# Seven half-size block products in place of eight for the gate and up tiles of four feed-forward stages

## The chip, the cores and the metric

The program runs on one core of one Trainium2 chip. The metric is device time in microseconds for one execution, the median of several runs. Before the change it is 3092.79 us (3 runs, 3091.29 to 3094.11).

## The reference

The reference is a two-block transformer on one sequence of 512 tokens and width 1024, all in float32. The part that the change touches is the feed-forward network of the first block, which stands before and after the mixer in each of its two layers:

```
gate = x @ W_gate            # [512, 1024] @ [1024, 2816]
up   = x @ W_up              # [512, 1024] @ [1024, 2816]
h    = silu(gate) * up
x    = layer_norm(ALPHA * x + 0.5 * (h @ W_down))    # W_down: [2816, 1024]
```

The second block has two more feed-forward networks of the same sizes (with an RMS norm) and a mixer with sparse attention. They are left as they are. The result must agree with float32 to a tolerance that a single reduced-precision product doesn't meet.

## The kernel before, in words

**Layout.** Features are on the 128 partitions, tokens along the free dimension. `x` is [128, 8, 528]: 8 tiles of 128 features (index k), 16 meta columns and 512 tokens. A weight piece is 128 output features by 1024 input features (8 blocks of 128x128, one for each k), 512 KB. The hidden width 2816 is 22 tiles (index f, `FT`), so a feed-forward stage has 44 pieces for gate and up, in the order gate 0, up 0, gate 1, up 1, and then 24 for the down product (8 output tiles m of 3 pieces each).

**Precision.** Every operand is split in two: `hi` is the value rounded to the format that TensorE takes (fp32r), `lo` is the rest. Every block product is three matmuls: w_hi·x_hi (L397), w_lo·x_hi (L400), w_hi·x_lo (L403), all into one PSUM bank. A piece in these stages is 8 x 3 = 24 matmuls of 512 columns, each with its own weight load.

**Who does what for a piece.** SyncE loads it into one of four raw buffers (L379), as soon as the piece four before has been split. ScalarE copies it to `w_hi` (`act_split`, L340), VectorE takes the rest to `w_lo` (`dve_split`, L351); four slots hold the split pieces. For hidden tile f ScalarE takes silu of the gate bank (L574), VectorE multiplies with the up bank (L596), ScalarE makes the high part of h (L578) and VectorE its low part (L606). GpSimd has no work in the gate and up part of these stages; it adds squares and sums near the norms (L735, L754, L1031) and splits weights in the mixers (L366).

**Order.** Each engine runs one fixed list of instructions, written out by the loops in `ffn_pe`, `ffn_act`, `ffn_dve`; semaphores carry the dependencies. Step s of these loops is one piece; splits run three pieces ahead (`AHEAD`). The first 3 or 5 pieces of a stage are taken together (`pe_group`) while the norm before still delivers x. `Prepare` makes small tables of the second block beside the first stage.

The stages by the trace of before: first-layer feed-forward `ffn1_0` 0 to 387 us, `mix_0`, `ffn2_0` from 617, `ffn1_1` from 992, `mix_1` from 1366, `ffn2_1` from 1598, and the second block from 1985.

## Time and profile before

| | |
|---|---|
| median of 3 runs | 3092.79 us |
| span of the profiled execution | 3090.1 us |
| TensorE matmul busy | 3043.6 us (98%), 16494 matmuls |
| VectorE busy | 1421.9 us (46%) |
| ScalarE busy | 1158.2 us (37%) |
| GpSimd busy | 379.7 us (12%) |
| moved by DMA | 269.62 MB, mean 87 GB/s |

The profiled execution is told by its span, from its first to its last instruction; the median of the timed runs is 2.7 us above that span. A matmul's record overlaps the next one, since the array is pipelined: what a matmul costs is the distance between the starts of two that follow each other, not its duration. The same holds to a smaller degree for VectorE and ScalarE, where the next instruction starts some 0.09 us before the record of the last one ends. "Idle before" with a name behind it says what ended a wait.

### The profile page before, as it was taken

Reading aid. Unit: us, or ns where it says so; the run is one execution under the profiler, and the core shown is the slowest. Engines: PE = TensorE matmul, PEld = TensorE weight load, DVE = VectorE, ACT = ScalarE, POOL = GpSimd, SP = SyncE. Lnnn points to the kernel's source line nnn. Section 1 sums busy time; section 2 is a strip of 40 time slices with the busy share of each in tenths; the row PEclk is TensorE's granted clock in tenths of the full one; section 3 lists DMA queues with packets and bytes.
Section 4 is the critical chain, followed back from the end, with each engine's and each line's share of the span. In section 5 each row is a group of like instructions: output and inputs, shape, how many; then the busy total and the mean of one; then the engine's idle time right before and its main releaser. Section 6 shows DMA issues by size and latency. Waiting matters only on the chain.

```text
span 3090.1 us, 39392 instructions
## 1 busy us (share of the span) xinstructions
PE 3043.6 (98%) x16494; PEld 2548.2 (82%) x16494; DVE 1421.9 (46%) x2120; ACT 1158.2 (37%) x1868; POOL 379.7 (12%) x319
## 2 busy tenths in 40 slices
PE   9999999999999999999999999899999999999999
PEld 7888877888888888887788888899999767788888
DVE  4333465653335333356583333744423766554432
ACT  3322376442223322146553221522223456543221
POOL 0000143300001000014320000200002323200000
PEclk9999999999999999999999999999999999999999
DMA  4223331132332322332123223222233211122232
GB/s 161 96 94 89 93 103 62 55 110 96 94 93 66 117 95 92 94 118 67 55 76 103 95 90 95 75 96 89 86 89 102 80 38 35 41 95 93 93 93 77
DMA packets 76496, 269.62 MB, mean 87 GB/s; under 512 B 8720, under 2 KB 9008, under 8 KB 76064
## 3 DMA queue, kind: packets, MB, share of 16 engines
q1 hardware_dynamic: 74448, 260.08, 26.3%
q0 software_dynamic: 1872, 7.04, 0.7%
q8 instruction: 130, 2.13, 0.3%
q14 instruction: 46, 0.38, 0.0%
HBM read 264.97 MB, written 2.11 MB: 86 GB/s over the span
## 4 chain that ended last, share of the span: by engine, by line
PE 90%; DVE 7%; ACT 2%; issue 1%; DMA 0%; SPq 0%; POOL 0%; DVEq 0%; ACTq 0%
PE psum L397 25%; PE psum L400 25%; PE psum L403 25%; PE psum L461 3%; PE psum L473 2%; PE psum L416 1%; PE psum L420 1%; PE psum L418 1%; PE psum L696 1%; PE psum L2840 1%; DVE z_sum L853 1%; DVE x L865 1%; DVE x L858 1%; DVE b_rank L3115 0%; PE psum L1881 0%
## 5 line engine op out<-in xcount | busy, mean ns | idle before, releaser
L351 DVE TENSOR_TENSOR w_lo<-w_raw,w_hi 128x1024 fp32r<-128x1024 f32 (+1 forms) x444 | 554.7, 1251 | 1260.5 <-ACT w_hi L340 1260.4
L397 PE MATMUL psum<-x_hi,w_hi 128*128 128x512 f32 (+1 forms) x2800 | 964.0, 368 | 1.1 <-ACT neg_mean L2911 0.8
L400 PE MATMUL psum<-x_hi,w_lo 128*128 128x512 f32 (+1 forms) x2800 | 949.8, 363 | 0.9 <-DVE w_lo L351 0.9
L403 PE MATMUL psum<-x_lo,w_hi 128*128 128x512 f32 (+1 forms) x2800 | 945.2, 362 | 0.1
L340 ACT CAST w_hi<-w_raw 128x1024 fp32r<-128x1024 f32 (+1 forms) x490 | 503.7, 1029 | 1172.7 <-PE psum L403 1137.1
L397 PEld LDWEIGHTS psum<-x_hi,w_hi 128*128 128x128 f32 x2800 | 500.0, 188 | 109.0 <-issue 18.6
L400 PEld LDWEIGHTS psum<-x_hi,w_lo 128*128 128x128 f32 x2800 | 499.6, 188 | 88.0 <-issue 4.8
L403 PEld LDWEIGHTS psum<-x_lo,w_hi 128*128 128x128 f32 x2800 | 500.4, 189 | 84.7 <-DVE x_lo L3349 0.4
L397 PE MATMUL psum<-h_hi_ffn,w_hi 128*128 128x512 f32 (+1 forms) x792 | 296.9, 375 | 0.0
L400 PE MATMUL psum<-h_hi_ffn,w_lo 128*128 128x512 f32 (+1 forms) x792 | 292.2, 369 | 0.0
L403 PE MATMUL psum<-h_lo_ffn,w_hi 128*128 128x512 f32 (+1 forms) x792 | 290.7, 367 | 0.0
L397 PEld LDWEIGHTS psum<-h_hi_ffn,w_hi 128*128 128x128 f32 x792 | 149.0, 188 | 28.6 <-issue 1.0
L403 PEld LDWEIGHTS psum<-h_lo_ffn,w_hi 128*128 128x128 f32 x792 | 148.8, 188 | 28.2
L400 PEld LDWEIGHTS psum<-h_hi_ffn,w_lo 128*128 128x128 f32 x792 | 148.6, 188 | 27.2 <-issue 1.0
L366 POOL TENSOR_TENSOR w_lo<-w_raw,w_hi 128x512 fp32r<-128x512 f32 x92 | 119.7, 1324 | 248.6 <-ACT w_hi L340 248.5
L397 PE MATMUL psum<-h_hi_b_ffn,w_hi 128*128 128x264 f32 (+2 forms) x550 | 148.6, 316 | 0.0
L400 PE MATMUL psum<-h_hi_b_ffn,w_lo 128*128 128x264 f32 (+2 forms) x550 | 148.1, 315 | 0.0
L403 PE MATMUL psum<-h_lo_b_ffn,w_hi 128*128 128x264 f32 (+2 forms) x550 | 147.7, 314 | 0.0
L1031 POOL TENSOR_TENSOR z_sum<-x 128x512 f32<-128x512 f32 x4 | 5.2, 1299 | 1054.7 <-DVE x L1003 1054.7
L578 ACT CAST h_hi_ffn<-hid 128x512 fp32r<-128x512 f32 x88 | 54.6, 621 | 163.8 <-DVE hid L596 163.8
L403 PEld LDWEIGHTS psum<-h_lo_b_ffn,w_hi 128*128 128x128 f32 x550 | 93.2, 188 | 7.1
L397 PEld LDWEIGHTS psum<-h_hi_b_ffn,w_hi 128*128 128x128 f32 x550 | 93.1, 188 | 7.0
(386 smaller groups left out, 3388.3 us busy)
## 6 DMA issues: line engine op xcount, KB each, us to landing
w_raw<-in_ffn_gu SPq DMA_DIRECT2D x176, 512.0 KB, 3.3
w_raw<-in_ffn_down SPq DMA_DIRECT2D x64, 512.0 KB, 3.5
w_raw<-in_w_in SPq DMA_DIRECT2D x44, 512.0 KB, 3.3
w_raw<-in_b_gate SPq DMA_DIRECT2D x44, 512.0 KB, 3.3
w_raw<-in_b_up SPq DMA_DIRECT2D x44, 512.0 KB, 3.3
w_raw<-in_b_down SPq DMA_DIRECT2D x32, 512.0 KB, 3.5
w_raw<-in_ffn_down SPq DMA_DIRECT2D x32, 384.0 KB, 3.1
w_raw<-in_b_in SPq DMA_DIRECT2D x24, 512.0 KB, 3.3
```

Of the source, the lines that this page charges most:

```text
L340: nc.scalar.copy(w_hi[s][:, 0:n], w_raw[r][:, 0:n]).then_inc(*w_high.inc(u))
L351: nc.vector.tensor_tensor(w_lo[s][:, 0:n], w_raw[r][:, 0:n], w_hi[s][:, 0:n].bitcast(F32), ALU.subtract).then_inc(*w_low_dve.inc(u))
L366: nc.gpsimd.tensor_tensor(w_lo[s][:, c], w_raw[r][:, c], w_hi[s][:, c].bitcast(F32), ALU.subtract).then_inc(*w_low_pool.inc((u, half)))
L397: nc.tensor.matmul(out, w_h, hi[:, c], start=first and i == 0, stop=False)
L400: nc.tensor.matmul(out, w_l, hi[:, c], start=False, stop=False)
L403: done = nc.tensor.matmul(out, w_h, lo[:, c], start=False, stop=final and i == n - 1)
L416: nc.tensor.matmul(out, w_h, hi[:, c], start=j == 0, stop=False)
L418: nc.tensor.matmul(out, w_l, hi[:, c], start=False, stop=False)
L420: done = nc.tensor.matmul(out, w_h, lo[:, c], start=False, stop=j == KT // 2 - 1)
L461: nc.tensor.matmul(out, w_h, x_part[:, c], start=first, stop=False, skip_group_check=True)
L473: done = nc.tensor.matmul(out, w_l, x_hi[:, k, c], start=False, stop=k == KT - 1, skip_group_check=True)
L578: nc.scalar.copy(h_hi[:, f - 1, cols], hid[(f - 1) % 2][:, cols]).then_inc(*h_high.inc(f - 1))
```

## The change

In the four feed-forward stages of the first block the hidden tiles f = 4 to 21 no longer compute gate and up by two pieces of full width. The input is cut into its first and second four k (1, 2), the tokens into two halves of 256 (a, b), and the weights of a tile pair into G1, G2 (gate) and U1, U2 (up). The four results are made from seven products instead of eight, each of 4 x 3 = 12 matmuls of 256 columns:

```
s1 = U1+U2    s2 = s1+G1    s4 = s2+G2    s3 = U1+G1            (VectorE, per f)
n1 = x1a-x1b  n2 = -n1-x2b  t3 = x2b-x1b  t4 = -n2-x2a          (VectorE, once per stage)
m1 = G1 x1a   m2 = G2 x2a   m3 = s4 x2b   m4 = U2 t4
m5 = s1 n1    m6 = s2 n2    m7 = s3 t3
gate_a = m1+m2          gate_b = (m1+m6) + (m5+m3)
up_b = -(m1+m6+m7)-m5   up_a = -(m1+m6+m7+m4)
```

m1, m6, m7 and m4 are summed in one PSUM bank, and ScalarE copies that bank out between them (p1 after m1, p2 after m6); m5 and m3 are summed in a second one (copy r after m5). VectorE joins the parts (`gate_a`, `gate_b`, `up_b`) and makes the first half of h. GpSimd makes the second half of h and the low part of all of h, and after the last tile adds x_hi and x_lo back to x, since t3 and t4 are kept in x's own memory. The four split slots get roles: sums (s1 and s3), gate, up, later (s2 and s4). The raw buffer of a gate piece is free after s3, that of an up piece after its low part. `Prepare` moves to earlier steps and other buffers, and the memory for descriptors of GpSimd's DMAs is set to 4096 bytes.

```diff
+COMBINED = {"ffn1_0": 4, "ffn2_0": 4, "ffn1_1": 4, "ffn2_1": 4}
...
-                    sp.wait_ge(*w_low(u - RAW_SLOTS))
+                    last = u - RAW_SLOTS
+                    sp.wait_ge(*(raw_read[last] if last in combined else w_low(last)))
...
+            def pe_product(self, name, f):
+                role, at, block, b = {
+                    "m1": ("gate", 0, "gate", self.p_bank(f)),
+                    "m2": ("gate", 1, "gate", self.q_bank),
+                    "m3": ("later", 1, "later", self.r_bank(f)),
+                    "m4": ("up", 0, "up", self.p_bank(f)),
+                    "m5": ("sums", 0, "s1", self.r_bank(f)),
+                    "m6": ("later", 0, "later", self.p_bank(f)),
...
+                opens = name in ("m1", "m2", "m5")
...
+                for f in range(first, FT + 1):
+                    if f <= last:
+                        pe.wait_ge(*(self.joined.at(("gate_b", f - 2)) if f >= first + 2
+                                     else self.direct_left(self.r_bank(f))))
+                        self.pe_product("m5", f)
+                    if f > first:
+                        pe.wait_ge(*self.copied.at(("p2", f - 1)))
+                        self.pe_product("m7", f - 1)
+                    if f <= last:
+                        pe.wait_ge(*(self.first_half.at(f - 3) if f >= first + 3
+                                     else self.direct_left(self.p_bank(f))))
+                        self.pe_product("m1", f)
+                        pe.wait_ge(*(self.joined.at(("gate_a", f - 1)) if f > first
+                                     else self.direct_left(self.q_bank)))
+                        self.pe_product("m2", f)
+                    else:
+                        fill()
+                    if f > first:
+                        pe.wait_ge(*self.joined.at(("up_b", f - 1)))
+                        self.pe_product("m4", f - 1)
+                    if f <= last:
+                        pe.wait_ge(*self.copied.at(("p1", f)))
+                        self.pe_product("m6", f)
+                        pe.wait_ge(*self.copied.at(("r", f)))
+                        self.pe_product("m3", f)
...
+                    if stored and f == first + 3:
+                        stored()
+                    if first <= f <= last:
+                        self.act_high("later", f)
+                    elif f > last:
+                        act_split(u_down + 1)
+                    if f > first:
+                        act.wait_ge(*self.joined.at(("gate_b", f - 1)))
+                        h = self.h[(f - 1) % 2][:, TOK]
+                        nc.scalar.activation(h, h, ACT.Silu).then_inc(*self.silu.inc(f - 1))
+                    if first <= f <= last:
+                        self.act_copy("r", f)
+                        self.act_high("s3", f)
+                        self.act_copy("p1", f)
+                    if f < last:
+                        self.act_high("s1", f + 1)
+                        self.act_high("gate", f + 1)
+                    elif f == last:
+                        act_split(u_down)
+                    if first <= f <= last:
+                        self.act_high("up", f)
+                    if f == first:
+                        hidden()
+                    elif f > first:
+                        self.act_hidden(f - 1)
+                    if first <= f <= last:
+                        self.act_copy("p2", f)
...
+                    if f > first:
+                        self.dve_join("gate_b", f - 1)
+                    if first <= f <= last:
+                        self.dve_low("later", f)
+                        self.dve_sum("s3", f)
+                    elif f > last:
+                        dve_split(u_down + 1)
+                    if f > first:
+                        self.dve_join("up_b", f - 1)
+                    if first <= f <= last:
+                        self.dve_low("s3", f)
+                    if f < last:
+                        self.dve_sum("s1", f + 1)
+                        self.dve_sum("s2", f + 1)
+                        self.dve_sum("s4", f + 1)
+                    if first <= f <= last:
+                        self.dve_join("gate_a", f)
+                    if f < last:
+                        self.dve_low("s1", f + 1)
+                        self.dve_low("gate", f + 1)
+                    elif f == last:
+                        dve_split(u_down)
+                    if f == first:
+                        hidden()
+                    elif f > first:
+                        self.dve_first_half(f - 1)
+                    if first <= f <= last:
+                        self.dve_low("up", f)
+                    if f == first:
...
+            def pool(self):
+                for f in range(self.f0, FT):
+                    h = self.h[f % 2]
+                    pool.wait_ge(*self.joined.at(("up_b", f)))
+                    pool.wait_ge(*self.silu.at(f))
+                    nc.gpsimd.tensor_tensor(h[:, self.b], self.up_b[:], h[:, self.b],
+                                            ALU.mult).then_inc(*self.second_half.inc(f))
+                    pool.wait_ge(*self.h_high.at(f))
+                    nc.gpsimd.tensor_tensor(
+                        self.h_lo[:, f, :], h[:, TOK], self.h_hi[:, f, :].bitcast(F32),
+                        ALU.subtract).then_inc(*self.h_low_pool.inc(f))
+                pool.wait_ge(*self.product_made.at(("m4", FT - 1)))
+                for k in range(KT):
+                    for part in self.entry.parts:
+                        pool.wait_ge(*self.entry.hi(k, part))
+                        pool.wait_ge(*self.entry.lo(k, part))
+                    nc.gpsimd.tensor_tensor(
+                        x[:, k, TOK], x_hi[:, k, TOK].bitcast(F32), x_lo[:, k, TOK].bitcast(F32),
+                        ALU.add).then_inc(*self.rebuilt.inc(k))
...
+                if half:
+                    half.pe(lambda: down_piece(0, 0))
...
+                    if half and s in (1, 4):
+                        half.act_turned(s // 4)
...
+                    if half and s == 1:
+                        half.dve_turned(0)
+                    if half and s in (2, 5):
+                        half.dve_turned_low(s // 4)
...
-    nc = bacc.Bacc("TRN2", target_bir_lowering=False, num_devices=1)
+    nc = bacc.Bacc("TRN2", target_bir_lowering=False, num_devices=1,
+                   dynamic_dma_scratch_size=4096)
```

The lists of instructions show what one pass holds. VectorE before, in `ffn1_0`, for one hidden tile (two weight pieces and one tile of h):

```order
L351 TENSOR_TENSOR w_lo0<-w_raw0,w_hi0 128x1024 [waits w_high]
L606 TENSOR_TENSOR h_lo_ffn1_0<-hid1,h_hi_ffn1_0 128x512 [waits h_high]
L351 TENSOR_TENSOR w_lo1<-w_raw1,w_hi1 128x1024 [waits w_high]
L596 TENSOR_TENSOR hid0<-hid0,psum 128x512 [waits w_used,ffn_silu]
L351 TENSOR_TENSOR w_lo2<-w_raw2,w_hi2 128x1024 [waits w_high]
```

VectorE now, in the same stage, from the s1 of tile f+1 to its `up_b` and on (`z_sum` holds p1 and p2, `neg_mean` r, `sq_sum` s1, `square` s2 and s4):

```order
L832 TENSOR_TENSOR square<-sq_sum,w_raw0 128x512 [waits c_sum,w_loaded0]
L832 TENSOR_TENSOR square<-square,w_raw0 128x512 [waits c_sum]
L844 TENSOR_TENSOR hid1<-psum,z_sum 128x256 [waits h_low_pool,c_copied,c_product]
L811 TENSOR_TENSOR w_lo0<-sq_sum,w_hi0 128x512 [waits c_high]
L811 TENSOR_TENSOR w_lo1<-w_raw0,w_hi1 128x1024 [waits c_high]
L866 SCALAR_TENSOR_TENSOR hid0<-psum,hid0 128x256 [waits ffn_silu,c_product]
L811 TENSOR_TENSOR w_lo2<-w_raw3,w_hi2 128x512 [waits c_high]
L849 TENSOR_TENSOR hid1<-psum,z_sum 128x256 [waits c_copied,c_product]
L811 TENSOR_TENSOR w_lo3<-square,w_hi3 128x1024 [waits c_high]
L832 TENSOR_TENSOR w_raw1<-w_raw1,w_raw0 128x512
L857 SCALAR_TENSOR_TENSOR up_b_ffn1_0<-psum,neg_mean 128x256 [waits c_second,c_product]
L811 TENSOR_TENSOR w_lo0<-w_raw1,w_hi0 128x512 [waits c_high]
```

Where four instructions served a tile, there are now thirteen: two of 1024 columns as before, seven of 512 and four of 256, and three of the waits are on ScalarE's work for the same tile.

GpSimd, which had nothing in this place, has two for each tile now:

```order
L913 TENSOR_TENSOR hid0<-up_b_ffn1_0,hid0 128x256 [waits ffn_silu,c_joined]
L916 TENSOR_TENSOR h_lo_ffn1_0<-hid0,h_hi_ffn1_0 128x512 [waits h_high]
```

The low part of h (L606 above) has moved here from VectorE. ScalarE now, for one tile (before it had two casts of 1024, one silu and one cast of 512):

```order
L749 CAST w_hi3<-square 128x1024 [waits c_product,c_sum]
L788 ACTIVATE hid1<-hid1 128x512 [waits c_joined]
L766 COPY neg_mean<-psum 128x256 [waits c_product]
L749 CAST w_hi0<-w_raw1 128x512 [waits c_product,c_sum]
L766 COPY z_sum<-psum 128x256 [waits c_product]
L749 CAST w_hi0<-sq_sum 128x512 [waits c_sum]
L749 CAST w_hi1<-w_raw2 128x1024 [waits c_product,w_loaded2]
L749 CAST w_hi2<-w_raw1 128x512 [waits c_product,w_loaded1]
L772 CAST h_hi_ffn1_0<-hid1 128x512 [waits c_second,c_first]
L766 COPY z_sum<-psum 128x256 [waits c_product]
```

The last two rows show where the high part of h stands: behind GpSimd's and VectorE's halves of h and ahead of p2, for which TensorE's m7 waits.

## Rows read from the trace of the kernel before

**Rows 1.** The page: busy tenths by slice, the granted clock, the chain by engine.
```profile
PE   9999999999999999999999999899999999999999
PEclk9999999999999999999999999999999999999999
PE 90%; DVE 7%; ACT 2%; issue 1%; DMA 0%; SPq 0%; POOL 0%; DVEq 0%; ACTq 0%
```
**Rows 2.** Windows: us, each engine's busy us (instructions), granted clock, DMA share, GB/s.
```profile
100.00:300.00 200.00, 200.00 (x865) 162.10 (x864) 64.66 (x71) 53.37 (x66) 1.29 (x1) 1.00 0.29 92
3073.00:3087.00 14.00, 14.00 (x121) 14.00 (x120) 0.52 (x2) 0.00 (x0) 0.00 (x0) 1.00 0.08 28
2000.00:2350.00 350.00, 350.00 (x2869) 350.00 (x2868) 133.94 (x156) 93.81 (x111) 9.12 (x5) 1.00 0.29 92
```
**Rows 3.** Timeline of TensorE at 200 and 3080 us: start, duration, engine, line.
```profile
200.08 0.39 PE L403 MATMUL psum<-x_lo,w_hi 128*128 128x512 f32 x1
200.31 0.39 PE L397 MATMUL psum<-x_hi,w_hi 128*128 128x512 f32 x1
...
3079.74 0.28 PE L400 MATMUL psum<-h_hi_b_ffn,w_lo 128*128 128x256 f32 x1
3080.44 0.28 PE L400 MATMUL psum<-h_hi_b_ffn,w_lo 128*128 128x256 f32 x1
```
**Rows 4.** Who waited for whom in 87 to 352 us: total us, times, longest.
```profile
DVE w_lo L351 <- ACT w_hi L340: 165.4, 49, 4.3
ACT w_hi L340 <- PE psum L403: 163.4, 49, 4.5
```
**Rows 5.** Timeline of VectorE at 2760 us (a stage with two more products).
```profile
2760.70 1.22 DVE L351 TENSOR_TENSOR w_lo<-w_raw,w_hi 128x1024 fp32r<-128x1024 f32 x1 [2.46 <-ACT w_hi L340]
2761.84 0.69 DVE L606 TENSOR_TENSOR h_lo_b_ffn<-hid,h_hi_b_ffn 128x512 fp32r<-128x512 f32 x1
2762.44 0.69 DVE L616 TENSOR_TENSOR hid<-psum,z_sum 128x512 f32<-128x512 f32 x1
...
2767.40 0.68 DVE L596 TENSOR_TENSOR hid<-hid,psum 128x512 f32<-128x512 f32 x1
2768.11 0.69 DVE L601 TENSOR_TENSOR hid<-hid,z_sum 128x512 f32<-128x512 f32 x1
```
**Rows 6.** Groups by line and form: busy, mean ns.
```profile
L858 DVE SCALAR_TENSOR_TENSOR x<-psum,x 128x256 f32<-128x256 f32 x96 | 36.9, 419 | 0.2
...
L2014 ACT CAST y_hi<-psum 128x256 fp32r<-128x256 f32 x16 | 5.9, 368 | 11.3 <-PE psum L1881 11.3
```
**Rows 7.** Timeline of ScalarE at 104 and 644 us.
```profile
104.65 1.05 ACT L340 CAST w_hi<-w_raw 128x1024 fp32r<-128x1024 f32 x1 [1.73 <-PE psum L403]
...
644.14 0.62 ACT L578 CAST h_hi_ffn<-hid 128x512 fp32r<-128x512 f32 x1 [1.89 <-DVE hid L596]
644.67 1.04 ACT L340 CAST w_hi<-w_raw 128x1024 fp32r<-128x1024 f32 x1
```
**Rows 8.** Timeline of VectorE and GpSimd where both work (285 to 288 us).
```profile
285.34 0.69 DVE L1003 SCALAR_TENSOR_TENSOR x<-x,psum 128x512 f32<-128x512 f32 x1 [2.30 <-PE psum L403]
286.48 2.01 DVE L351 TENSOR_TENSOR w_lo<-w_raw,w_hi 128x1024 fp32r<-128x1024 f32 x1 [0.45 <-ACT w_hi L340]
...
286.11 1.29 POOL L1031 TENSOR_TENSOR z_sum<-x 128x512 f32<-128x512 f32 x1 [210.87 <-DVE x L1003]
```
**Rows 9.** GpSimd's products by line: duration ns min/median/max.
```profile
L754 POOL TENSOR_TENSOR sq_sum<-sq_sum,square x36: 732/750/1228, 591.6 to 2718.4; 128x256 f32<-128x256 f32 x36
L366 POOL TENSOR_TENSOR w_lo<-w_raw,w_hi x92: 1260/1287/2270, 405.5 to 2697.7; 128x512 fp32r<-128x512 f32 x92
```
**Rows 10.** SyncE's weight loads in 640 to 960 us: issue to landing, us.
```profile
DMA to landing us min/median/max: 3.0/3.3/4.7
```
**Rows 11.** Entry of `ffn1_1`: chain of TensorE and timeline of ScalarE.
```profile
1007.53 9.27 PE psum L473 x40
...
1003.18 5.00 ACT L820 ACTIVATE x<-x,gains 128x512 f32<-128x512 f32 x8
```

More of the change, by code:

```diff
@@ L218, in slot_plan @@
             own[u] = (SPLIT_SLOTS + i, first[name] - (OUT_PAIRS + 1 if from_mixer else 2))
-    slot, before, ring = [], [], []
+    combined = combined_pieces(first)
+    slot, before, roles = {}, {}, {}
+    ring = [(i, None) for i in range(SPLIT_SLOTS)]
     for u in range(len(plan)):
         if u in own:
-            slot.append(own[u][0])
-            before.append(own[u][1])
-        else:
-            slot.append(len(ring) % SPLIT_SLOTS)
-            before.append(ring[-SPLIT_SLOTS] if len(ring) >= SPLIT_SLOTS else None)
-            ring.append(u)
-    return slot, before
+            slot[u], before[u] = own[u]
+        elif u not in combined:
+            slot[u], before[u] = ring.pop(0)
+            ring.append((slot[u], u))
+        elif combined[u] not in roles:
+            name = combined[u]
+            roles[name] = dict(zip(("sums", "gate", "up", "later"), ring))
+            at, last = {role: i for role, (i, _) in roles[name].items()}, FT - 1
+            ring = [(at["gate"], (name, "m2", last)), (at["later"], (name, "m3", last)),
+                    (at["sums"], (name, "m7", last)), (at["up"], (name, "m4", last))]
+    return slot, before, roles
 def pool_pieces(plan, first):
@@ L513, in held @@
             def held(i):
-                before = [j for j in range(i) if bank(j) == bank(i)]
+                before = [j for j in range(i) if bank(j) == bank(i)
+                          and not n_direct <= j < n_up]
+                if i >= n_up and f0 < FT and (i - n_up) < 4:
+                    return [half.bank_left(bank(i))]
                 if before:
@@ L520, in hidden, with down_outs @@
             def hidden(k):
-                return h_hi[:, k, :], h_lo[:, k, :], h_high.at(k), h_low.at(k)
+                return h_hi[:, k, :], h_lo[:, k, :], h_high.at(k), (
+                    h_low if k < f0 else h_low_pool).at(k)
+            def down_outs(outs):
+                return [(out, slice(c.start - h_first, c.stop - h_first)) for out, c in outs]
+            half = Combined(tag, u0, f0, own, reader, bank, entry, hid, silu, h_high, h_low,
+                            h_low_pool, h_hi, h_lo) if f0 < FT else None
             def ffn_pe():
                 pe_group(u0, wide, [bank(i) for i in range(group)], entry, group, held)
-                for i in range(group, n_up):
-                    if prepare and i in (10, 14):
-                        prepare.pe((i - 10) // 4)
+                for i in range(group, n_direct):
+                    if prepare and i in (3, 6):
+                        prepare.pe((i - 3) // 3)
                     pe_wait_banks(held(i))
@@ L580, in ffn_act, with dve_hidden @@
+                    if 2 <= s and s % 2 == 0:
+                        act_hidden(f - 1)
+                if half:
+                    half.act(lambda: act_hidden(f0 - 1), u_down,
+                             prepare.act_stored if prepare else None)
+                for s in range(n_up, n_up + 3 * KT - 2):
+                    act_split(u0 + s + AHEAD)
+                    if s == n_up and not half:
+                        act_hidden(FT - 1)
                     if s > n_up:
                         leave.act_after(*divmod(s - n_up, 3))
+            def dve_hidden(f):
+                dve.wait_ge(*silu.at(f))
+                dve.wait_ge(*w_used.at(u0 + 2 * f + 1))
+                h = view(hid[f % 2][:, cols])
+                made = nc.vector.tensor_tensor(h, h, product(bank(2 * f + 1)), ALU.mult)
+                if entry.late:
+                    made.then_inc(*dve_own.inc())
+                    dve.wait_ge(*dve_own.done())
+                    h = hid[f % 2][:, cols]
+                    made = nc.vector.tensor_tensor(h, h, z_sum[:, cols], ALU.mult)
+                made.then_inc(*gated.inc(f))
```

415 lines of the change are left out of this document (356 added, 59 removed).

## The prediction

> **What bounds the kernel now.** I read the page first: TensorE is busy in every slice at the full clock, and 90% of the chain that ended last is TensorE [rows 1]. The question is then what a matmul costs, and that is read from the distance of starts. Between 100 and 300 us, inside a feed-forward stage, there are 865 matmuls in 200 us; two of them stick out over the edges, so 200 / 863 = 0.2317 us each, with no idle time [rows 2, 3]. The list of waits says the same from the other side: ScalarE waits 163 us for TensorE and VectorE as long for ScalarE [rows 4]. Nothing but TensorE limits the gate and up part, and the helpers have room: of 200 us VectorE is busy 65, ScalarE 53 and GpSimd 1 [rows 2].
>
> **TensorE's term.** Before, a hidden tile is 2 pieces of 24 matmuls of 512 columns: 48 x 0.2317 = 11.12 us. Now it is 7 x 12 = 84 matmuls of 256 columns. Each loads its own weights, 0.188 us by its record, so the question is whether 256 columns are too few to hide that. At 3073 us the trace has the same kind of work: 121 matmuls in 14 us, less two at the edges, 0.1177 us each, and six steps in 0.70 us [rows 2, 3]. The second block runs for 350 us on halves of 264 columns: 350 / 2867 = 0.1221 us, a weight load each, full clock [rows 2]. So weight loads overlap at this width, and half the columns cost 51% and not 50%. What the trace doesn't have is a change of bank every 12 matmuls at this width. From below 0.1177, from above 0.1221, the row of 264 columns; I take 0.118, close to the row of the same width. 84 x 0.118 = 9.91 us, 1.21 less for a tile, and 4 x 18 = 72 tiles: 87.1 us (89 at 0.1177, 62 at 0.1221).
>
> The Trainium skill (TensorE: Matmul & The Clock Gate, Back-to-back issue gap) gives sustained distances of 81 ns for 128 columns and 131 ns for 512. By a straight line between them, an estimate of mine from that page, 256 columns cost 98 ns, and the change would lose (84 x 98 - 48 x 131) x 72 = 140 us. The rows disagree: 512 columns take 231.7 ns in this kernel and 256 take 117.7.
>
> **Whether the helpers keep pace.** This decides how much of the 87 us stays. VectorE goes from four instructions for a tile to thirteen. By starts, an instruction of 1024 columns takes 1.14 us and one of 512 0.60; one that waits for the result of the one before it comes 0.71 after it instead of 0.60 [rows 5]; one of 256 columns with PSUM has a record of 0.42 [rows 6] and, with the same 0.09 of overlap as the others, 0.33. So 2 x 1.14 + 7 x 0.60 + 2 x 0.11 + 4 x 0.33 = 8.0 us for a tile, of 9.91. ScalarE has 2 x 0.96 + 5 x 0.53 + 3 x 0.28 = 5.4 us, its records of 1.05, 0.62 and 0.37 less the same overlap [rows 6, 7]. Both fit by their sums; the chain that runs through them is closer.
>
> GpSimd's part is new here: 0.75 us for 256 columns and 1.29 for 512 [rows 9]. The trace shows what it does to VectorE: at 286.11 GpSimd starts a sum of 1.29 us, at 286.48 VectorE starts a low part that takes 2.01 instead of 1.23, so it moved only from about 287.26, 1.15 after GpSimd's start [rows 8]. The product of 256 should hold VectorE back for about 0.75 - 0.14 = 0.6.
>
> The Trainium skill (SBUF — State Buffer, Who interferes with whom) calls this an exclusive port: a VectorE instruction with two SBUF inputs and a GpSimd instruction that reads SBUF block each other, one with a single SBUF input is left alone. It speaks against this change, as nine of the thirteen have two SBUF inputs.
>
> I follow the chain once around, from VectorE's first half of h (`L866`) of a tile at 0, with hand-overs of 0.03 us between VectorE and ScalarE and, as [rows 8] have it, 0.08 to GpSimd (285.34 + 0.69 to 286.11).
> - ScalarE's high part of h 0.45 to 1.08; copy p2 from 0.98, its record 0.37 long; cast of `later` 1.25 to 2.30.
> - GpSimd's low part of h starts at 1.16 and lets VectorE go at 2.31. So VectorE's low part of `later` starts at 2.33 on either account; the low part of h costs nothing here, because VectorE waits for ScalarE's cast in the same time.
> - low of `later` to 3.47, s3 to 4.07, `up_b` to 4.41 (record 4.49). GpSimd's half of h starts at 4.57 and frees VectorE at 5.18. ScalarE's cast of s3 would have been ready at 4.85, so GpSimd costs 0.33 here.
> - low of s3 5.78, s1 6.49, s2 7.20, s4 7.80, `gate_a` 8.13, low of s1 8.73, low of gate 9.87; then the next first half of h.
>
> The loop is 9.87 us, against TensorE's 9.91. TensorE therefore stays the bound, with almost no margin. Its other waits have slack: m7 wants p2 1.4 us after the start of a tile's period, `up_b` comes some 2 us before m4, the gate's low part 4 us before m1. The raw buffers have it too: an up piece's buffer is free at 1.0 in this loop, its next load takes 3.3 us, at most 4.7 [rows 10], and s1 reads it at 5.8. Late loads of over 4.7 us would be felt and are rare.
>
> **Entry of the stages.** Beside the four direct tiles VectorE gets sixteen instructions (4 sums and 4 low parts, twice; 10 us) and ScalarE eight casts (4.2 us). In `ffn1_1` ScalarE frees x at 1008.2 and TensorE ends its group of five pieces at 1016.8 [rows 11]; three direct pieces of 5.56 us follow, so the first product is due at 1033.5. Walking VectorE's list by the durations above, s1's low part is ready at 1032.0 and the gate's at 1033.2, in time. But then the high part of `later` needs the slot of the last direct piece (free at 1033.7), and behind it come the high part of tile 3's h, late since VectorE still has it in its list, and then p2: 1043.5, where m7 wants it at 1042.0. With the low part of s1 0.4 late, that is 1.6 us lost; in `ffn1_0`, which starts without a group, 0.9. Together 3 x 1.6 + 0.9 = 5.7 us. At least 0 if ScalarE has more room than I found, at most about 3 us a stage.
>
> **What costs nothing.** The rebuilding of x, eight additions of 1.29 us after the last m4, has 11 us until the first sum for the norm needs tile 0, and 15 us for each further tile. The first down piece stands between the last m7 and m4 and covers `up_b` with 5.6 us; if that cover were missing, a stage would lose 1 to 2 us. The smaller memory for GpSimd's descriptors is not shown by any row: below 0, above some 5 us in the mixers, whose tables are loaded by that queue; I take 0. `Prepare` takes as many steps as before.
>
> **The sum**, against the profiled execution: 3090.1 - 87.1 + 5.7 = 3008.7 us; the median of the runs stands 2.7 above that span, so 3011.4 us.
>
> **Rivals.**
> - GpSimd's lock takes more. If it holds to the end of its record and is given over once more, 0.14 twice is added, and the loop becomes 10.15 to 10.2; the helpers are the bound, 0.27 us more for each of 72 tiles: 19 us, 3031 us. For it: the loop and TensorE's period differ by 0.04 us only, and some of GpSimd's records are far over their median [rows 9]. Against: 2.01 in [rows 8] shows the earlier release.
> - Matmuls of 256 columns with a bank change every 1.4 us cost 0.1221, as the rows of 264 do: 25 us back, 3036 us. Against it, those rows have 8 more columns, and at (0.2317 - 0.1177) / 256 us for a column that is 0.0036 of the 0.0044.
> - TensorE loses nothing at the entries and holds 0.1177: 3004 us. For it: the 1.6 us are what is left after some 25 instructions of a walk, and 0.06 too much for each would be all of it.
> - Slower than before, by one mechanism: GpSimd's two instructions take what their longest records show, 2.27 and 1.23 us [rows 9], because VectorE is between them and the port each time. Then VectorE starts `later` 0.98 later and the low part of s3 0.48 later, and the loop is 9.87 + 1.46 = 11.33 against 11.12 before: 72 x 0.21 + 5.7 = 21 us more, 3114 us. It decides from a loop of 11.04, that is from 1.17 us of such delay a tile. Against it: in the walk GpSimd starts both times while VectorE waits for ScalarE and nothing is in its way.
> - The change doesn't do what it says: the seven products have the count of matmuls above by the list, so TensorE's work falls in any case; only the waits can keep it.
>
> **Chances and range.** Forecast (3005 to 3017) 0.55; nothing lost at the entries 0.08; lock 0.22; bank changes 0.05; slower 0.04; something else between 3040 and 3085, such as late loads, 0.06. Range 3002 to 3036. A measurement of this kernel tells about 0.2% from no change, 6 us: faster 0.95, same 0.01, slower 0.04.
>
> **What would show it.** Right: in 130 to 320 us TensorE's matmuls stand 0.118 apart with idle time only at a stage's entry, a tile every 9.9 us; VectorE some 80% busy there; GpSimd's half of h starting right behind `up_b`, with VectorE's low part of s3 longer than 0.69; each stage 20 us shorter. Wrong: idle time of TensorE ahead of m7 (waiting for ScalarE's copy p2) in every tile, which would be the loop; distances of 0.122 inside a product, which would be the matmul's price; a low part of `later` over 1.4 us, which would be the lock in the place where I hide it. A period above 11.04 would make it slower.

## The result, and the profile after

The changed kernel takes 3016.02 us (median of 4 runs, 3015.58 to 3017.09) against 3092.07 (4 runs, 3091.29 to 3094.11): ratio 0.9755, 95% interval 0.9741 to 0.9768, so 76 us faster. The forecast was 3011.4 us, 4.6 below. The profiled execution has a span of 3014.3 us. Its page, first engines and then the chain that ended last (shares of the span), against [rows 1]:

```profile
PE 2961.4 (98%) x19086; PEld 2616.7 (87%) x19086; DVE 1835.2 (61%) x2832; ACT 1348.4 (45%) x2332; POOL 583.4 (19%) x495
...
PE 88%; DVE 8%; ACT 2%; issue 1%; DMA 0%; SPq 0%; POOL 0%; DVEq 0%; ACTq 0%
```

TensorE still makes up most of the chain that ended last, 88% instead of 90%; VectorE has 8% instead of 7%. The same 120 us inside `ffn1_0`, before and then after (columns: start:end, length, busy us and count of TensorE, its weight loads, VectorE, ScalarE, GpSimd, granted clock, DMA share, GB/s):

```profile
110.00:230.00 120.00, 120.00 (x520) 97.29 (x519) 40.16 (x44) 35.40 (x44) 0.00 (x0) 1.00 0.28 92
```
```profile
110.00:230.00 120.00, 120.00 (x1014) 119.97 (x1013) 102.88 (x156) 68.32 (x121) 24.43 (x24) 1.00 0.35 107
```

There are 1014 matmuls instead of 520 in the same time, so 256 columns cost little over half of 512. VectorE went from 33% to 86% busy. TensorE looks full, and yet one distance in each tile is too long. These are ScalarE's copy p2 (`L766`), TensorE's weight loads and then its matmuls at the start of an m7 (start, duration):

```profile
84.56 0.37 ACT L766 COPY z_sum<-psum 128x256 f32<-128x256 f32 x1
```
```profile
84.82 0.19 PEld L682 LDWEIGHTS psum<-t_lo_ffn,w_hi 128*128 128x128 f32 x1
84.98 0.19 PEld L677 LDWEIGHTS psum<-x_turned,w_hi 128*128 128x128 f32 x1
85.09 0.19 PEld L680 LDWEIGHTS psum<-x_turned,w_lo 128*128 128x128 f32 x1
```
```profile
84.93 0.28 PE L682 MATMUL psum<-t_lo_ffn,w_hi 128*128 128x256 f32 x1
85.05 0.32 PE L677 MATMUL psum<-x_turned,w_hi 128*128 128x256 f32 x1
85.20 0.28 PE L680 MATMUL psum<-x_turned,w_lo 128*128 128x256 f32 x1
```

The first weight load of m7 comes 0.16 us after the one before it and the second matmul 0.15 (up to 0.20 in other tiles) instead of 0.118. No idle time is shown, since records overlap; the delay is seen only in the starts. p2 ends at 84.56 + 0.37 = 84.93, just before that weight load. So m7 waits in every tile by a few hundredths, and the period of a tile, from one m7 to the next, is 9.964 us, in all four stages within 0.002, where 84 undisturbed distances of 0.11825 would be 9.933.

p2 comes late because ScalarE and VectorE hand work to each other in a loop, once per tile, and that loop takes longer than TensorE's work for the tile. This is one turn of it on VectorE (start, duration, and in brackets the idle time before and what ended it):

```profile
83.58 0.42 DVE L866 SCALAR_TENSOR_TENSOR hid<-psum,hid 128x256 f32<-128x256 f32 x1
83.92 0.68 DVE L811 TENSOR_TENSOR w_lo<-w_raw,w_hi 128x512 fp32r<-128x512 f32 x1
85.03 0.42 DVE L849 TENSOR_TENSOR hid<-psum,z_sum 128x256 f32<-128x256 f32 x1 [0.43 <-ACT z_sum L766]
85.91 1.22 DVE L811 TENSOR_TENSOR w_lo<-square,w_hi 128x1024 fp32r<-128x1024 f32 x1 [0.46 <-ACT w_hi L749]
87.05 0.68 DVE L832 TENSOR_TENSOR w_raw<-w_raw 128x512 f32<-128x512 f32 x1
87.66 0.42 DVE L857 SCALAR_TENSOR_TENSOR up_b_ffn<-psum,neg_mean 128x256 f32<-128x256 f32 x1
88.43 1.02 DVE L811 TENSOR_TENSOR w_lo<-w_raw,w_hi 128x512 fp32r<-128x512 f32 x1 [0.35 <-ACT w_hi L749]
89.37 0.68 DVE L832 TENSOR_TENSOR sq_sum<-w_raw 128x512 f32<-128x512 f32 x1
90.15 0.69 DVE L832 TENSOR_TENSOR square<-sq_sum,w_raw 128x512 f32<-128x512 f32 x1
90.88 0.69 DVE L832 TENSOR_TENSOR square<-square,w_raw 128x512 f32<-128x512 f32 x1
91.49 0.41 DVE L844 TENSOR_TENSOR hid<-psum,z_sum 128x256 f32<-128x256 f32 x1
91.82 0.68 DVE L811 TENSOR_TENSOR w_lo<-sq_sum,w_hi 128x512 fp32r<-128x512 f32 x1
92.42 1.21 DVE L811 TENSOR_TENSOR w_lo<-w_raw,w_hi 128x1024 fp32r<-128x1024 f32 x1
93.56 0.41 DVE L866 SCALAR_TENSOR_TENSOR hid<-psum,hid 128x256 f32<-128x256 f32 x1
```

From `L866` at 83.58 to the next at 93.56 it is 9.98 us by these rounded starts. The turns of the four stages lie between 9.95 and 9.98 and are 9.963 on average, which is the period. The names are those of reused memory: `square` holds s4, `sq_sum` s1, `w_raw` at 87.05 s3. GpSimd's two instructions stand beside them: the low part of h (`L916`) in VectorE's wait for the cast of `later`, and half of h (`L913`) behind `up_b`.

```profile
84.73 1.29 POOL L916 TENSOR_TENSOR h_lo_ffn<-hid,h_hi_ffn 128x512 fp32r<-128x512 f32 x1 [5.80 <-ACT h_hi_ffn L772]
88.15 0.74 POOL L913 TENSOR_TENSOR hid<-up_b_ffn,hid 128x256 f32<-128x256 f32 x1 [2.12 <-DVE up_b_ffn L857]
```

At a stage's entry TensorE waits twice, in the second tile, and in all four stages alike (541, 541, 540, 534 ns and 1359, 1359, 1361, 1369 ns instead of 118 between the two matmuls concerned). The weight loads in `ffn1_0`:

```profile
62.40 0.19 PEld L680 LDWEIGHTS psum<-t_hi_ffn,w_lo 128*128 128x128 f32 x1 [0.47 <-DVE w_lo L811]
...
65.05 0.19 PEld L677 LDWEIGHTS psum<-x_turned,w_hi 128*128 128x128 f32 x1 [1.29 <-ACT z_sum L766]
```

That is 0.42 us for the low part of s1 (m5) and 1.24 for p2 (m7). The matmul behind each of these two also starts 0.22 us after the one before it instead of 0.118, another 0.10 each time. So the entry costs 1.87 us a stage, 7.5 in all. From the start of the first m5's first matmul to the start of the last m4's last one it is 186.6 us in each stage.

### The profile page after: what moved, and what is told of

The parts are those of the page before. It is cut to its first block, busy times and chain, and to the rows that moved or that the text cites. A ratio compares the mean times of both kernels' runs of the same rounds, so it can differ in the third digit from the quotient of the medians.

```text
span 3014.3 us, 46624 instructions
## 1 busy us (share of the span) xinstructions
PE 2961.4 (98%) x19086; PEld 2616.7 (87%) x19086; DVE 1835.2 (61%) x2832; ACT 1348.4 (45%) x2332; POOL 583.4 (19%) x495
## 3 DMA queue, kind: packets, MB, share of 16 engines
q1 hardware_dynamic: 74448, 260.08, 28.4%
## 4 chain that ended last, share of the span: by engine, by line
PE 88%; DVE 8%; ACT 2%; issue 1%; DMA 0%; SPq 0%; POOL 0%; DVEq 0%; ACTq 0%
PE psum L424 17%; PE psum L427 17%; PE psum L430 17%; PE psum L677 8%; PE psum L682 8%; PE psum L680 7%; PE psum L488 4%; PE psum L500 2%; PE psum L447 1%; PE psum L443 1%; PE psum L1208 1%; PE psum L445 1%; PE psum L3356 1%; DVE z_sum L1365 1%; DVE w_lo L811 0%
## 5 line engine op out<-in xcount | busy, mean ns | idle before, releaser
L424 PE MATMUL psum<-x_hi,w_hi 128*128 128x512 f32 (+1 forms) x1648 | 511.2, 351 | 2.6 <-ACT neg_mean L3427 1.8
L427 PE MATMUL psum<-x_hi,w_lo 128*128 128x512 f32 (+1 forms) x1648 | 493.2, 340 | 0.9 <-DVE w_lo L377 0.9
L430 PE MATMUL psum<-x_lo,w_hi 128*128 128x512 f32 (+1 forms) x1648 | 491.2, 339 | 0.1
L424 PEld LDWEIGHTS psum<-x_hi,w_hi 128*128 128x128 f32 x1648 | 283.1, 188 | 58.4 <-issue 18.4
L427 PEld LDWEIGHTS psum<-x_hi,w_lo 128*128 128x128 f32 x1648 | 282.8, 188 | 37.8 <-issue 4.8
L430 PEld LDWEIGHTS psum<-x_lo,w_hi 128*128 128x128 f32 x1648 | 282.8, 189 | 35.9 <-DVE x_lo L3865 0.8
L677 PE MATMUL psum<-x_hi,w_hi 128*128 128x256 f32 x864 | 242.7, 281 | 0.0
L682 PE MATMUL psum<-x_lo,w_hi 128*128 128x256 f32 x864 | 242.0, 280 | 0.0
L680 PE MATMUL psum<-x_hi,w_lo 128*128 128x256 f32 x864 | 241.7, 280 | 0.0
L811 DVE TENSOR_TENSOR w_lo<-w_raw,w_hi 128x512 fp32r<-128x512 f32 (+1 forms) x216 | 208.3, 964 | 27.2 <-ACT w_hi L749 27.2
L916 POOL TENSOR_TENSOR h_lo_ffn<-hid,h_hi_ffn 128x512 fp32r<-128x512 f32 x72 | 93.3, 1296 | 412.1 <-ACT h_hi_ffn L772 412.1
```

What stands on the lines that cost most here:

```text
L424: nc.tensor.matmul(out, w_h, hi[:, c], start=first and i == 0, stop=False)
L427: nc.tensor.matmul(out, w_l, hi[:, c], start=False, stop=False)
L430: done = nc.tensor.matmul(out, w_h, lo[:, c], start=False, stop=final and i == n - 1)
L677: nc.tensor.matmul(self.out(b), w_h, hi, start=opens and k == 0, stop=False, skip_group_check=True)
L680: nc.tensor.matmul(self.out(b), w_l, hi, start=False, stop=False, skip_group_check=True)
L682: done = nc.tensor.matmul(self.out(b), w_h, lo, start=False, stop=k == HALF_K - 1, skip_group_check=True)
```

## The experiments

Medians are in us with the range of the runs; the ratio is to the kernel before, run beside it. "Period" is the time from one m7 to the next and "products" the length of the product phase in `ffn1_0` (the 186.6 us above), both in us from the trace of one execution.

| kernel | median (range, runs) | ratio (95%) | span | period | products |
|---|---|---|---|---|---|
| changed kernel | 3016.02 (3015.58-3017.09, 4) | 0.9755 (0.9741-0.9768) | 3014.3 | 9.964 | 186.6 |
| e1_p2_first | 3009.52 (3008.68-3011.37, 4) | 0.9735 (0.9722-0.9748) | 3007.4 | 9.942 | 184.9 |
| e2_half_on_dve | 3016.39 (3015.06-3019.31, 4) | 0.9758 (0.9744-0.9771) | 3013.8 | 9.933 | 186.1 |
| e3_low_on_dve | 3018.63 (3015.72-3020.05, 5) | 0.9761 (0.9748-0.9775) | 3017.3 | 9.961 | 186.6 |
| e4_pool_twice | 3051.88 (3051.40-3052.36, 2) | 0.9871 (0.9853-0.9889) | 3051.1 | 10.503 | 195.3 |
| e5_best | 3009.60 (3007.53-3011.58, 4) | 0.9734 (0.9720-0.9747) | 3010.3 | 9.933 | 184.3 |
| e6_both_on_dve | 3016.19 (3014.43-3017.81, 5) | 0.9755 (0.9742-0.9769) | 3013.8 | 9.933 | 186.1 |
| e7_two_stages | 3056.36 (3055.70-3058.14, 4) | 0.9886 (0.9872-0.9899) | 3056.8 | 9.964 | 186.6 |
| e8_before_scratch | 3092.47 (3090.80-3093.07, 10) | 1.0002 (0.9993-1.0011) | 3091.4 | | |
| e9_roles | 3012.40 (3011.23-3015.23, 4) | 0.9743 (0.9727-0.9759) | 3011.3 | 9.961 | 185.3 |

**e1_p2_first: ScalarE copies p2 ahead of the high part of h.**

```diff
+                    if first <= f <= last:
+                        self.act_copy("p2", f)
                     if f == first:
                         hidden()
                     elif f > first:
                         self.act_hidden(f - 1)
-                    if first <= f <= last:
-                        self.act_copy("p2", f)
```

> ScalarE copies p2 before it makes the high part of the last tile's h, and not after it. Theory A (the loop): in the changed kernel the period of 9.96 us is set by the chain from VectorE's first half of h over ScalarE's high part, p2 and the cast of `later` back to VectorE, and TensorE feels it at m7, whose first matmul comes 0.167 us after the one before instead of 0.118. With p2 ahead, m7 waits for nothing that comes from VectorE: 84 x 0.118 = 9.91 us a tile, 72 x 0.05 = 3.8 us less, and the wait of 1.24 us ahead of the first m7 of each stage goes too, 5.0 us: 3016.0 - 8.8 = 3007 us. Theory B (TensorE's own price): the 0.05 us are what a change of bank or a wait on a semaphore costs there, whoever is early: they stay, only the 5.0 us go: 3011 us.

ScalarE in this kernel (`z_sum` at 91.08 is p2):

```profile
89.61 1.56 ACT L749 CAST w_hi<-w_raw 128x1024 fp32r<-128x1024 f32 x2
91.08 0.36 ACT L766 COPY z_sum<-psum 128x256 f32<-128x256 f32 x1
93.01 0.62 ACT L772 CAST h_hi_ffn<-hid 128x512 fp32r<-128x512 f32 x1 [1.57 <-DVE hid L866]
93.53 1.04 ACT L749 CAST w_hi<-square 128x1024 fp32r<-128x1024 f32 x1
```

p2 now lies in ScalarE's own wait, and the cast of `later` follows the high part of h at once. Both waits of m7 are gone, in the tiles and at the entry, as theory A had it; the wait of m5 at the entry stays (536, 535, 536, 535 ns). A stage's products take 1.7 us less; four of them make 6.8, and the medians differ by 6.5. The instruction order on ScalarE alone was worth that.

It is less than theory A's 8.8 us, since the period is 9.942 and not TensorE's own 9.933: the loop is still the bound. VectorE's low part of `later` and GpSimd's low part of h show why:

```profile
94.61 1.48 DVE L811 TENSOR_TENSOR w_lo<-square,w_hi 128x1024 fp32r<-128x1024 f32 x1 [0.70 <-ACT w_hi L749]
```
```profile
93.71 1.30 POOL L916 TENSOR_TENSOR h_lo_ffn<-hid,h_hi_ffn 128x512 fp32r<-128x512 f32 x1 [5.81 <-ACT h_hi_ffn L772]
```

ScalarE hands over `later` 0.27 us earlier in the turn than in the changed kernel, but GpSimd is still at its low part of h, and VectorE's record grows from 1.22 to 1.48. So GpSimd takes back nearly all that the shorter way over ScalarE gives; in most tiles the low part of s1 reaches m5 up to 0.05 us late. This edit together with the low part of h on VectorE was not run.

**e2_half_on_dve: the half of h that GpSimd makes goes to VectorE, behind `up_b`.**

```diff
-                    nc.gpsimd.tensor_tensor(h[:, self.b], self.up_b[:], h[:, self.b], ...
+                        self.dve_second_half(f - 1)
```

> The second half of h is multiplied by VectorE right behind up_b and not by GpSimd; GpSimd keeps the low part of h. Theory A: GpSimd's product of 0.74 us holds back VectorE's low part of s3 by 0.33 us in each loop. On VectorE the product takes 0.40 us in time in which it waited for ScalarE's cast of s3, so the loop falls from 9.96 to about 9.65, TensorE's 9.91 is the bound: 3016.0 - 3.8 = 3012 us; the waits at the entries stay. Low part of s3 by its record 0.68 again. Theory B: 3016, as m7's 0.05 us stay. Theory C (VectorE's load counts, not its chain): 0.40 us more for each of 72 tiles, 3045 us.

VectorE (`L866` at 106.25 is the moved product here; the first half is `L874` in this kernel):

```profile
105.79 0.42 DVE L857 SCALAR_TENSOR_TENSOR up_b_ffn<-psum,neg_mean 128x256 f32<-128x256 f32 x1
106.25 0.42 DVE L866 TENSOR_TENSOR hid<-up_b_ffn,hid 128x256 f32<-128x256 f32 x1
106.59 0.68 DVE L811 TENSOR_TENSOR w_lo<-w_raw,w_hi 128x512 fp32r<-128x512 f32 x1
107.19 0.68 DVE L832 TENSOR_TENSOR sq_sum<-w_raw 128x512 f32<-128x512 f32 x1
...
112.84 0.42 DVE L849 TENSOR_TENSOR hid<-psum,z_sum 128x256 f32<-128x256 f32 x1 [0.44 <-PE psum L682]
```

From `up_b` to s1 it is 1.40 us here and 1.71 in the changed kernel: the product fits into the wait for ScalarE's cast of s3, and the low part of s3 takes 0.68 instead of 1.02. The helper loop is 0.3 shorter, nothing waits in the steady part any more, and VectorE waits for TensorE instead (last row). The period is 9.933, which is TensorE's own. That is 0.031 us for each of the 16 periods from the first m7 of a stage to the last: 0.5 us a stage, as the products show, and 2.0 in all, where theory A had 3.8 because it took 9.91 for TensorE. The medians don't show it (3016.4 against 3016.0, with ranges of 4 and 1.5 us): in the trace of this kernel the time between the two down products of the second block, where the instructions are the same, is 2.0 us longer (596.5 against 594.5; the last section comes back to this).

**e3_low_on_dve: the low part of h goes to VectorE, two tiles late, ahead of `gate_b`.**

```diff
-                    nc.gpsimd.tensor_tensor(self.h_lo[:, f, :], h[:, TOK], ..., ALU.subtract)
+                    if f > first + 1:
+                        self.dve_h_low(f - 2)
```

> The low part of h is made by VectorE ahead of gate_b and not by GpSimd; GpSimd keeps the second half of h. Theory A: VectorE has 0.43 us ahead of gate_b and 0.46 ahead of the low part of `later` in which it waits for ScalarE. The low part of h (0.60 from start to start) fits into the two together, so nothing is lost and nothing gained: 3016 us, within 2. Theory C (VectorE's load counts): 72 x 0.60 = 43 us more, 3059 us.

The period is 9.961 and the products take 186.6 us, both as in the changed kernel: in this kernel GpSimd's 1.29 us under the cast of `later` cost nothing. The median is 2.6 us above that of the changed kernel, a little outside the 2 that were expected. The 3 us more of the span lie between the same two down products (597.5 us against 594.5).

**e4_pool_twice: GpSimd makes its half product twice for each tile** (the first time into memory that is overwritten).

```diff
+                    nc.gpsimd.tensor_tensor(self.h_lo[:, f, WIDTH:], self.up_b[:], h[:, self.b],
+                                            ALU.mult).then_inc(*pool_own.inc())
+                    pool.wait_ge(*pool_own.done())
```

> GpSimd multiplies the second half of h twice, the first time into memory that is written over later, so GpSimd has some 0.89 us more a tile right behind up_b. Theory A with the lock: VectorE's low part of s3 can't start while either reads. If both stand ahead of it, the loop grows by 0.89: 72 x 0.89 = 64 us, 3080 us; if VectorE gets its low part in between, the second one holds back s1 by about 0.6: 43 us, 3059 us. Theory D (no lock, only latency): the second half of h is still ready 4 us before ScalarE takes it, so no change, 3016 us.

VectorE, and then GpSimd, in one tile:

```profile
98.68 0.42 DVE L857 SCALAR_TENSOR_TENSOR up_b_ffn<-psum,neg_mean 128x256 f32<-128x256 f32 x1
99.45 1.01 DVE L811 TENSOR_TENSOR w_lo<-w_raw,w_hi 128x512 fp32r<-128x512 f32 x1 [0.35 <-ACT w_hi L749]
100.38 1.22 DVE L832 TENSOR_TENSOR sq_sum<-w_raw 128x512 f32<-128x512 f32 x1
101.71 0.69 DVE L832 TENSOR_TENSOR square<-sq_sum,w_raw 128x512 f32<-128x512 f32 x1
```
```profile
99.17 0.74 POOL L913 TENSOR_TENSOR h_lo_ffn<-up_b_ffn,hid 128x256 fp32r<-128x256 f32 x1 [2.12 <-DVE up_b_ffn L857]
99.99 1.07 POOL L916 TENSOR_TENSOR hid<-up_b_ffn,hid 128x256 f32<-128x256 f32 x1
```

The two engines alternate instruction by instruction: the low part of s3 waits for GpSimd's first product, GpSimd's second (1.07 instead of 0.74) for the low part of s3, and s1 (1.22 instead of 0.68) for that one. The 0.54 us of s1 are the whole of the period's growth, 9.964 to 10.503. This is the branch of theory A in which VectorE gets its low part in between. Its 43 us were too many: the loop sets 16 periods of a stage and not 18, and 64 x 0.54 = 34.6 us; the medians differ by 35.9. m7 now waits visibly, for p2, in all 11 tiles that begin between 110 and 230 us (total, times, longest):

```profile
PEld psum L677 <- ACT z_sum L766: 5.7, 11, 0.5
```

So the helper loop is the bound, and a tile's time follows it one for one in this run.

**e5_best: e1 and e2 together, and the slots of `later` and `up` exchanged** (`dict(zip(("sums", "gate", "later", "up"), ring))`), so that the first `later` needs an older slot.

> Three edits together: p2 ahead of the high part of h (as in the first experiment), the second half of h on VectorE (as in the second), and the slots of `later` and `up` exchanged, so that the first cast of `later` waits for the last but one direct tile and not for the last. Theory A: every tile takes TensorE's own 9.933 us, 0.031 less than in the changed kernel, 2.2 us; the 1.24 us ahead of m7 and the 0.42 us inside m5 at each entry go, 5.0 and 1.7 us: 3016.0 - 8.9 = 3007 us. Theory E (the entry is short of VectorE time altogether, and not of the slot): the 0.42 us stay or turn up at another product, 3009 us, as in the first experiment.

The entry waits are gone (0.07 us is left in `ffn2_0`), the period is TensorE's own, and a stage's products take 184.3 us, 2.3 less than in the changed kernel (9.3 us for four): 1.87 of the entry and 0.5 of the periods. The median is 3009.60, 6.4 less, no better than e1. The profiled execution, the slowest of the four (3011.58), loses 4.1 us again between the two down products of the second block, 598.6 us against 594.5 with the same instructions (last section).

**e6_both_on_dve: both of GpSimd's shares on VectorE** (the edits of e2 and e3).

> Nothing of h is made by GpSimd: VectorE multiplies the second half of h behind up_b and makes the low part of h ahead of gate_b. Theory A: VectorE has 8.1 + 0.4 + 0.6 = 9.1 us of work in a period of 9.93, all of the additions where it waited for ScalarE; the loop without the 0.33 us of GpSimd's lock is below 9.93, so TensorE is the bound: a period of 9.933, 72 x 0.031 = 2.2 us less than the changed kernel, 3014 us, which means that GpSimd's part of the change brings nothing. Theory C (VectorE's load counts): 1.0 us more for each of 72 tiles less the slack, over 3050 us.

The period is 9.933 and the products take 186.1 us, as in e2; the median is 3016.19, 2 above the 3014 expected, and as in e2 the trace has 2.1 us more between the two down products of the second block. GpSimd brings the changed kernel nothing. VectorE has room for both, because each falls into one of its waits for ScalarE; TensorE is the bound without GpSimd's help too.

**e7_two_stages: products only in `ffn1_0` and `ffn2_0`.**

```diff
-COMBINED = {"ffn1_0": 4, "ffn2_0": 4, "ffn1_1": 4, "ffn2_1": 4}
+COMBINED = {"ffn1_0": 4, "ffn2_0": 4}
```

> The scheme in two stages (ffn1_0, ffn2_0), the other two by whole tiles as before. Each stage with the scheme saves 18 x (11.12 - 9.964) - 1.66 = 19.1 us by its parts. If the stages are independent and nothing else of the change costs or saves: 3091.5 - 38.3 = 3053 us. If something fixed comes with the change (other buffers, the memory of the descriptors), the two kernels don't stand at equal distances from 3091.5 and 3016.0.

The median is 3056.36, 3 us above the 3053 expected. Against 3091.4, the median of before beside it, the first two stages bring 35 us, and the other two 40 more: 18 and 20 us for each, where by their parts it is 18 x (11.12 - 9.964) less 1.87 of the entry, 18.9. The distances are not equal, so by this test alone a fixed cost of 5 us is possible. The traces don't show one. The products take 186.6 us in both stages of this kernel too, and the stretches at half the clock (last section) add up to 24.0 us in before, 28.4 here and 20.8 in the changed kernel. Counted at half, the differences are 2.2 and 3.8 us, an estimate, and with them the two distances would be 37.3 and 36.5.

**e8_before_scratch: the kernel before with the smaller memory for descriptors** (`dynamic_dma_scratch_size=4096`).

> The kernel before with nothing but the memory for descriptors of GpSimd's DMAs at 4096 bytes. I took 0 for this part, with 5 us as upper end: 3091.5 us, and at most 3096 if GpSimd's queue has to wait for descriptors in the mixers, where its loads of tables then land later than 391 and 2381 us.

3092.47 against 3091.44, ratio 1.0002 (0.9993 to 1.0011): no difference, where the interval leaves room for some 3 us.

**e9_roles: the slots of `later` and `up` exchanged, alone.**

> Only the slots of `later` and `up` exchanged in the changed kernel. Theory S (the slot is what makes the entry late): the first cast of `later` no longer waits for the last direct tile, VectorE's list behind it comes about 1 us earlier, and both the 0.42 us inside the second m5 and the 1.24 us ahead of the first m7 go: 6.6 us less, with the later periods at 9.964 as before: 3009 us. Theory P (the copy p2 behind the high part of tile 3 is a cause by itself): only the 0.42 us go, the wait ahead of m7 stays at 0.8 to 1.2 us: 3014 us.

The median is 3012.40, 3.6 us below the changed kernel and between the two accounts; neither is right alone. In `ffn1_0` and `ffn1_1` the wait of m5 is gone and that of m7 shrinks from 1.24 to 0.46 us:

```profile
63.28 0.19 PEld L677 LDWEIGHTS psum<-x_turned,w_hi 128*128 128x128 f32 x1 [0.50 <-ACT z_sum L766]
```

But in `ffn2_0` and `ffn2_1` m7 still waits 1.25 us, and their products take 186.6 and 186.1 us. What p2 stands behind is the same in all stages, the high part of tile 3's h on ScalarE, which waits for VectorE's product of that tile (`L1076`); in `ffn2_0`:

```profile
648.75 0.62 ACT L1038 CAST h_hi_ffn<-hid 128x512 fp32r<-128x512 f32 x1 [2.09 <-DVE hid L1076]
```

So what is late there is VectorE's list. With the new slot the low part of the first s1 starts 2.74 and 1.85 us before the first m5 in `ffn1_0` and `ffn1_1`, but only 0.44 and 0.91 in `ffn2_0` and `ffn2_1`, and m7's wait shrinks only where this lead is long. The place of p2 (e1) takes the m7 wait away in all four stages; the slot takes that of m5 away in three of four (in `ffn2_0` the first m5 waits 0.18 us and the second 0.12).

## Why the prediction was right, point by point

- **TensorE's term.** It was right in kind, and the gain in it 1.6 us too large. 0.118 was taken; 0.11825 is what TensorE does when nothing holds it (period 9.933 / 84, in e2, e5 and e6). 72 x (11.12 - 9.933) = 85.5 instead of 87.1. The change of bank every 12 matmuls costs next to nothing (0.119 at a change, 0.118 elsewhere, in e2); the upper bound of 0.1221 belonged to the 264 columns. The straight line between the figures of the Trainium skill (TensorE: Matmul & The Clock Gate, Back-to-back issue gap) would have had the change lose. The 131 ns that the Trainium skill gives there for 512 columns don't hold here: in before it is 231.7.
- **The helper loop.** The walk gave 9.87, the trace 9.96 on average (9.98 in the turn shown). Point by point in that turn, from `L866` at 0: p2 at 0.98 (walk 0.98), cast of `later` at 1.25 (1.25), its low part 2.33 (2.33), s3 3.47 (3.47), `up_b` 4.08 (4.07), GpSimd's half 4.57 (4.57), s1 5.79 (5.78). What the walk lacks comes behind it: s2 starts 0.78 after s1 and s4 0.73 after s2, where the walk has 0.71 for both after [rows 5]. So "TensorE stays the bound, with almost no margin" failed: the loop is the bound by 0.031 us for each of 64 periods, 2.0 us in all, as e2 shows by taking 0.3 out of it. The prediction's own sign for this, TensorE waiting for p2 ahead of m7 in every tile, did come, by a few hundredths.
- **GpSimd's lock.** 0.33 forecast on the low part of s3, 1.02 - 0.68 = 0.34 measured; the low part of h is free in this kernel, as e3 shows, though no longer once p2 stands ahead (1.48 instead of 1.22 in e1). The rival that the lock takes 0.14 twice more fell. The exclusive port of the Trainium skill (SBUF — State Buffer, Who interferes with whom) agrees with e4: a second 256-column product costs VectorE 0.54 us.
- **Entries.** 5.7 forecast, 7.5 measured. The three stages with a group have 1.87 us instead of 1.6, at the two places that the walk had named (low part of s1 0.42 late; p2 late for m7, 1.24). The 0.9 for `ffn1_0` failed as a step: it has 1.87 too. How far VectorE was ahead does differ (the low part of the first s1 starts 2.74 us before the first m5 in `ffn1_0`, 0.92, 1.93 and 0.89 in the others), but the first cast of `later` waits for the last direct piece and starts 0.25 us after the first m5 in all four, and everything behind it has the same times. With another slot the lead does count (e9).
- **What costs nothing.** At the exit nothing waits for the rebuilding of x, and m4 waits for nothing behind the down piece. The memory for descriptors costs nothing that e8 can tell. No wait in the products ends with a load.
- **The sum.** 3008.7 + 1.6 (matmul) + 2.0 (loop) + 1.8 (entries) = 3014.1; the span is 3014.3. That so little is left is luck in part: between the two down products of the second block the changed kernel is 2.3 us shorter than before (594.5 against 596.8) with the same instructions, and behind `ffn1_0` a drop of the clock costs it some 1.6 that e1 doesn't have (last section). The median stands 1.7 above this span, not 2.7: 3016.0.

The mechanism was as forecast in TensorE's work, the lock and the places of the entry waits, and wrong in which of the two bounds wins: a loop walked to 0.1 us can't tell between bounds 0.04 apart. It hardly mattered, since near the crossing both give the same time. The three terms were each too low by 1.6 to 2.0 us, all the same way, 5.4 us together; the median, 1.0 us closer to the span than taken, gives some of it back.

The version to use is e1's: one line moved on ScalarE, 3009.5 us, 6.5 below the changed kernel and 82 below the one before. Putting half of h on VectorE and exchanging the slots (e5) shortens the products by another 0.6 us a stage in the trace, but not the median measured.

## What to carry to other kernels

Where TensorE's work per tile falls, walk the helpers' loop by starts, hand-overs and dependent starts before trusting the new period, and compare it with TensorE's: what is over comes back one for one, for every tile between the first and the last (e4). Look at each engine's wait in that loop as free room: an instruction of another chain put there (p2 before the high part of h) costs no time of its own, and one put behind it may be what TensorE waits for. Moving a fitting instruction to GpSimd buys nothing if VectorE waits there anyway, and costs VectorE the shared port. That cost can hide in another wait and come out when this wait is taken away, as in e1.

## What the runs showed of the hardware

**TensorE's clock drops in different places from one trace to the next.** In every trace the granted clock is 0.5, so 1.2 of 2.4 GHz, for a few stretches of 3.4 or 6.8 us, always behind places where TensorE was idle part of the time (mixers, norms, the last matmuls), never in the products. One of them in the changed kernel, behind `ffn1_0`, ahead of it and behind it:

```profile
424.00:428.00 4.00, 2.14 (x13) 1.54 (x12) 1.44 (x4) 3.53 (x13) 0.21 (x1) 1.00 0.45 131
428.30:431.50 3.20, 3.20 (x12) 2.21 (x10) 1.49 (x2) 0.05 (x1) 0.00 (x0) 0.50 0.00 0
432.00:436.00 4.00, 4.00 (x34) 2.76 (x33) 3.71 (x7) 2.27 (x6) 2.58 (x2) 1.00 0.00 0
```

12 matmuls in 3.2 us, 0.27 each, against 34 in 4 us behind it. TensorE was busy for 2.14 of the 4 us ahead. In e1, whose work comes 2.4 us earlier here, the same place keeps the full clock, and from the end of that stage's down product to the first m5 of `ffn2_0` it takes 278.8 us instead of 280.4:

```profile
421.00:425.00 4.00, 2.75 (x18) 2.13 (x17) 2.05 (x4) 2.91 (x12) 0.83 (x1) 1.00 0.46 130
425.00:429.00 4.00, 3.38 (x18) 2.68 (x19) 2.17 (x2) 1.53 (x3) 0.00 (x0) 1.00 0.02 5
```

In e5 there is a stretch of 6.8 us in the second block that the changed kernel doesn't have:

```profile
2598.50:2605.50 7.00, 7.00 (x23) 5.66 (x24) 1.56 (x3) 1.83 (x6) 0.00 (x0) 0.51 0.00 0
```

From the end of the second block's first down product to the start of its second one it takes 596.8 us in before, 594.5 in the changed kernel, 595.6 in e1 and 598.6 in e5, with the same instructions. Only one execution of each kernel was traced. The executions of one kernel differ too: the five of e3 have a mean granted clock of 0.994 to 0.997 and take 3015.7 to 3020.1 us. Why a drop falls in one place and not in another wasn't tested; that it moves with the phase of the work is a guess. For the reader of such medians it means that 2 to 4 us outside the changed part come and go, and that a gain of 2 us is read from the period in the trace, not from the median.

**The port between VectorE and GpSimd goes over at each instruction, both ways.** In e4, where each has a further instruction ready, neither runs twice in a row, and GpSimd's record grows as well, from 0.74 to 1.07 us, while it waits. How much the port costs depends on what VectorE would have waited for: 1.29 us of GpSimd's work cost nothing in the changed kernel (e3) and 0.26 us in e1.
